# Cached attention pages with four neighbouring tokens to a partition, asked for and refilled in groups of four

## What is computed

```
k_past = cache_k[l, page_table].reshape(dec_b, past, 4, 128)      # past = 16 pages of 128 tokens
s = concat(q . k_past, q . k_new)                                 # per head and map
w = softmax(s * scale + bias)  of map 1  -  lam * the same of map 2
out = w[past] . v_past + w[new] . v_new
```

## Time and profile before

| what | us |
|---|---|
| median of 3 runs | 1985.19 |
| lowest and highest of them | 1980.44, 1985.21 |
| the profiled execution, its own time | 1986.06 |
| the profiled execution, its span from first to last instruction | 1984.5 |
| TensorE matmul busy | 1809.7 |
| weight loads of TensorE busy | 1656.1 |
| vector engine busy | 945.9 |
| scalar engine busy | 498.9 |
| key stretch, value stretch | 303 to 498, 498 to 612 |

### The profile page before, as it was taken

One profiled execution on the slowest core, in us unless ns is written; L12 is line 12 of the kernel. 1 busy time (PEld: TensorE's weight loads), 2 busy tenths in 40 slices (PEclk: granted clock), 3 DMA queues, 4 the chain that ended last, 5 costly groups with the idle time before them and its releaser, 6 DMA issues.

```text
span 1984.5 us, 32041 instructions
## 1 busy us (share of the span) xinstructions
PE 1809.7 (91%) x12995; PEld 1656.1 (83%) x12995; DVE 945.9 (48%) x1145; ACT 498.9 (25%) x861; POOL 117.3 (6%) x145
## 2 busy tenths in 40 slices
PE   6879998989988978898989879999999999999993
PEld 6779995656557968697779759999999999999982
DVE  5315888876765358422252393432323432333445
ACT  5111115666556221402431241110000010000122
POOL 2000001000220001001000020000000000000000
PEclk9889999999999989998999989999999999999995
DMA  5411216756785114213321121121111111111113
GB/s 177 134 44 59 69 64 204 204 166 199 247 300 188 64 46 145 107 43 127 128 86 43 42 88 43 43 63 43 42 43 42 44 63 43 43 42 37 48 44 131
DMA packets 137100, 187.80 MB, mean 95 GB/s; under 512 B 7720, under 2 KB 99050, under 8 KB 136486
## 3 DMA queue, kind: packets, MB, share of 16 engines
q1 hardware_dynamic: 122670, 121.47, 20.1%
q0 software_dynamic: 14192, 64.53, 9.2%
q10 hardware_dynamic: 144, 0.52, 0.1%
HBM read 166.17 MB, written 20.74 MB: 94 GB/s over the span
## 4 chain that ended last, share of the span: by engine, by line
PE 82%; DVE 7%; ACT 6%; issue 3%; DMA 2%; POOL 0%; SPq 0%; DVEq 0%; POOLq 0%; ACTq 0%
PE PS L1704 20%; PE PS L1705 19%; PE PS L1706 19%; PE PS L1694 7%; PE PS L1903 2%; PE PS L1925 2%; PE PS L1949 2%; DMA bias_rows<-BVEC 2%; PE PS L1824 2%; PE PS L2194 2%; ACT KTS L726 1%; PE PS L1986 1%; PE PS L1719 1%; PE PS L2215 1%; DVE Y L1225 1%
## 5 line engine op out<-in xcount | busy, mean ns | idle before, releaser
L1704 PE MATMUL PS<-XH,WH 128*128 128x352 f32 x1968 | 637.3, 324 | 18.8 <-ACT ST L726 18.8
L1705 PE MATMUL PS<-XL,WH 128*128 128x352 f32 x1968 | 632.4, 321 | 0.0
L1706 PE MATMUL PS<-XH,WL 128*128 128x352 f32 x1968 | 631.9, 321 | 0.0
L1125 DVE CAST WH<-RAW 128x1024 fp32r<-128x1024 f32 x126 | 94.2, 748 | 696.2 <-PE PS L1706 670.7
L1704 PEld LDWEIGHTS PS<-XH,WH 128*128 128x128 f32 x1968 | 370.4, 188 | 19.1 <-ACT ST L726 19.1
L1705 PEld LDWEIGHTS PS<-XL,WH 128*128 128x128 f32 x1968 | 371.1, 189 | 0.0
L1706 PEld LDWEIGHTS PS<-XH,WL 128*128 128x128 f32 x1968 | 370.2, 188 | 0.0
L1266 DVE SCALAR_TENSOR_TENSOR CY<-GP,DW,CY 128x1024 f32<-128x1024 f32 x124 | 158.5, 1278 | 1.0 <-DVE CY L1269 1.0
L1127 DVE TENSOR_TENSOR WL<-RAW,WH 128x1024 fp32r<-128x1024 f32 x126 | 156.5, 1242 | 4.3
L1704 PE MATMUL PS<-HH,WH 128*128 128x352 f32 x462 | 149.0, 323 | 0.0
L1705 PE MATMUL PS<-HL,WH 128*128 128x352 f32 x462 | 148.1, 321 | 0.0
(11 more groups left out here) (336 smaller groups left out, 2317.2 us busy)
## 6 DMA issues: line engine op xcount, KB each, us to landing
PG<-in_cache_k SPq DMA_DIRECT2D x128, 256.0 KB, 3.0
PG<-in_cache_v SPq DMA_DIRECT2D x64, 256.0 KB, 4.0
PG<-in_cache_v POOLq DMA_DIRECT2D x64, 256.0 KB, 4.2
RAW<-in_w_gate SPq DMA_DIRECT2D x22, 512.0 KB, 4.0
RAW<-in_w_up SPq DMA_DIRECT2D x22, 512.0 KB, 5.2
RAW<-in_w_in SPq DMA_DIRECT2D x20, 512.0 KB, 6.0
h_spill<-H POOLq DMA_DIRECT2D x2, 4224.0 KB, 11.9
H<-h_spill POOLq DMA_DIRECT2D x2, 4224.0 KB, 13.7
```

Source lines behind the costliest of these rows:

```text
L1125: dve.tensor_copy(WH[v % 2][:, :, :], raw).then_inc(hi_done, 1)
L1704: pe.matmul(out, WH[u][:, k, :], xh[:, k, cols], start=(k == 0), stop=False)
L1705: pe.matmul(out, WH[u][:, k, :], xl[:, k, cols], start=False, stop=False)
L1706: mm = pe.matmul(out, WL[u][:, k, :], xh[:, k, cols], start=False, stop=(k == kt - 1))
```

## The change

A page is read as 32 runs of four tokens, 8 KB each, to 32 partitions: page slot s goes to partitions 32 * (s mod 4) and the 31 behind it, into the four column blocks 4 * (s div 4) to the one 3 further. Four pages together fill the four column blocks on 128 partitions. What TensorE calls slot r is then column block r: every fourth token of each of the four pages of its group. Sums over tokens don't depend on the order, and keys and values have the same one. The near tokens are now on rows 96 to 127 of the last four column blocks, so EDGE is added there, in the same order of tokens.

Since a column block holds parts of four pages, TensorE waits for all four of a group, and a page may be overwritten only when all four column blocks of its group are used. There are 4 landing semaphores of each kind instead of 8, each for four slots. In the value stretch two of a group's pages come from SyncE and two from GpSimd, so every value page waits for both.

```diff
+        def page_rows(slot):
+            return PG[32 * (slot % 4):32 * (slot % 4) + 32, slot // 4 * 4:slot // 4 * 4 + 4, :]
+        def page_of(cache, page):
+            rows = cache[0].rearrange("n (i s) h d -> n i s (h d)", s=4)[ds(page, 1), :, :, :]
+            return rows.rearrange("n i s d -> (n i) s d")
...
-        pg_in = [sem(f"pg_in{i}") for i in range(PAGES // 2)]
-        vg_in = [sem(f"vg_in{i}") for i in range(PAGES // 2)]
+        pg_in = [sem(f"pg_in{i}") for i in range(PAGES // 4)]
+        vg_in = [sem(f"vg_in{i}") for i in range(PAGES // 4)]
...
-                src = cache[0].rearrange("n s h d -> n s (h d)")[ds(page, 1), :, :].rearrange("n s d -> (n s) d")
-                sp.dma_start(PG[:, slot, :], src).then_inc(pg_in[slot // 2], 16)
+                sp.dma_start(page_rows(slot), page_of(cache, page)).then_inc(pg_in[slot // 4], 16)
...
-                        sp.wait_ge(k_turned, PAGES * (n - 1) + r + 1)
+                        sp.wait_ge(k_turned, PAGES * (n - 1) + r // 4 * 4 + 4)
...
-                        sp.wait_ge(v_used, PAGES * (b - 1) + r + 1)
+                        sp.wait_ge(v_used, PAGES * (b - 1) + r // 4 * 4 + 4)
                     else:
-                        sp.wait_ge(k_turned, PAGES * (DB - 1) + r + 1)
+                        sp.wait_ge(k_turned, PAGES * (DB - 1) + r // 4 * 4 + 4)
...
-                        pool.wait_ge(v_used, PAGES * (b - 1) + r + 1)
+                        pool.wait_ge(v_used, PAGES * (b - 1) + r // 4 * 4 + 4)
...
-                    pool.dma_start(PG[:, r, :], src.rearrange("n s d -> (n s) d")).then_inc(vg_in[r // 2], 16)
+                    pool.dma_start(page_rows(r), page_of(io["cache_v"], page)).then_inc(vg_in[r // 4], 16)
...
-                dve.tensor_tensor(SD[:, g, (PAGES - 1) * P:PAGES * P], SD[:, g, (PAGES - 1) * P:PAGES * P], EDGE[:, :],
-                                  ALU.add).then_inc(sm_v, 1)
+                near = SD[:, g, (PAGES - 4) * P:PAGES * P].rearrange("p (s c) -> p s c", s=4)[:, :, 96:P]
+                dve.tensor_tensor(near, near, EDGE[:, :].rearrange("p (i s) -> p s i", s=4), ALU.add).then_inc(sm_v, 1)
...
-                pe.wait_ge(pg_in[r // 2], 32 * (n // PAGES) + 32)
+                pe.wait_ge(pg_in[r // 4], 64 * (n // PAGES) + 64)
...
-                if r % 2 == 0:
-                    pe.wait_ge(pg_in[r // 2], 32 * DB + 16 * (n // PAGES) + 16)
-                else:
-                    pe.wait_ge(vg_in[r // 2], 16 * (n // PAGES) + 16)
+                pe.wait_ge(pg_in[r // 4], 64 * DB + 32 * (n // PAGES) + 32)
+                pe.wait_ge(vg_in[r // 4], 32 * (n // PAGES) + 32)
```

More of the change, by code:

```diff
@@ L652, in _ @@
                     if b:
-                        pool.wait_ge(v_used, PAGES * (b - 1) + r + 1)
+                        pool.wait_ge(v_used, PAGES * (b - 1) + r // 4 * 4 + 4)
                     else:
-                        pool.wait_ge(k_turned, PAGES * (DB - 1) + r + 1)
+                        pool.wait_ge(k_turned, PAGES * (DB - 1) + r // 4 * 4 + 4)
                     page = pool.value_load(PT[:, PAGES * b + r:PAGES * b + r + 1], min_val=0, max_val=n_pages - 1)
-                    src = io["cache_v"][0].rearrange("n s h d -> n s (h d)")[ds(page, 1), :, :]
-                    pool.dma_start(PG[:, r, :], src.rearrange("n s d -> (n s) d")).then_inc(vg_in[r // 2], 16)
+                    pool.dma_start(page_rows(r), page_of(io["cache_v"], page)).then_inc(vg_in[r // 4], 16)
             pool.wait_ge(h_spilled, 16)
```

## The result

| | before | after |
|---|---|---|
| median of 4 runs, us | 1985.2 | 2015.67 |
| lowest and highest | 1980.44, 1986.15 | 2012.56, 2017.23 |
| profiled execution, us | 1986.06 | 2017.23 |
| its span | 1984.5 | 2015.4 |

The changed kernel takes 1.0156 times as long (95% interval 1.0135 to 1.0178), 30.5 us more. The prediction was 2008, with a range from 1987 to 2022. Medians and ratios of the experiments leave out three disturbed executions (one of e3, two of e8; 2327 to 3601 us).

What follows compares the result with a forecast made beforehand. TensorE was taken as nearly always busy, page transfers hidden beside it with little room in the value stretch. 21.3 + 2.5 - 1.2 = +22.6 us on 1986.06 gave 2008.7, so 2008 by the median; range 1987 to 2022.

Steps and rivals of the forecast that it cites:

- The mechanism that decides: Page transfers: landing on 32 partitions instead of 128, a page takes 1.16 us at about 226 GB/s.
- nearly all after 540: Sign of being right: transposes and products wait for pages, nearly all after 540 us.
- The value stretch: +21.3: Value stretch: 112 pages at 1.16 us after 501.9 end the last products at 632.9 instead of 611.65, +21.3 us.
- the first group's +2.5: Key stretch start: first transposes wait for four pages instead of two; +2.5 us, between 0 and 4.
- from there the transfers don't stop: Value stretch from 501.9 us: buffers wait for data, so pages follow without a gap at 1.16 us each.
- Refill by four: Key stretch: buffers are asked for up to three pages later, but 17 us of cover remain; nothing lost.
- -1.2: After the value stretch: the last slot's weights, waited for 1.23 us before, are no longer late; -1.2 us.
- The near-token add: Same 128x128 elements, 0.292 us, twice, with a split column pattern; cost 0, at most 0.6 us.
- Rival 1: Value stretch: both SBUF halves are written at once, faster than 270 GB/s; 1983 to 1999 us, chance 0.15.
- Rival 2: Value stretch: the halves overlap in part, 1.0 to 1.1 us a page; 1990 to 2001 us, chance 0.12.
- Rival 3: Page transfers are worse than the rows, 1.37 us a page, key stretch stalling too; 2032 us, chance 0.07.
- Rival 4: Page transfers: descriptors still move 2 KB, not 8 KB; the forecast holds, only packet counts would tell; no chance given.

Runs made afterwards that it cites:

- e3: Changed kernel with pages 1 and 2 of each group swapped, so the two queues write different halves of the SBUF in the value stretch; 2006.5 us.
- e8: From e1, key pages wait by two and refill singly, groups of four for value pages alone, all pages on 128 partitions; 1988.5 us.
- e6: Changed kernel with its 32-partition key pages, but value pages on 128 partitions, one token each; waits and refills by four stay; 1992.5 us.
- e4: Changed kernel with a page's 32 runs of 8 KB on every fourth partition of all 128; 1992.0 us.
- e12: Changed kernel with a page's 32 runs of 8 KB on every second partition of one half; 2016.5 us.
- e5: Changed kernel with a page as 64 runs of 4 KB on 64 neighbouring partitions of one half, buffers in groups of two; 1997.1 us.
- e11: e5 with another issue order: in the value stretch SyncE takes the first pair of each four pages, GpSimd the second; 1999.1 us.
- e9: Kernel before the change, with groups of four for key pages' waits and refills alone, all pages on 128 partitions; 1986.1 us.
- e1: Changed kernel's waits and refills by four, but pages on 128 partitions in 2 KB runs as before the change; 1990.9 us.
- e2: Changed kernel with four runs of 2 KB per partition instead of one of 8 KB, on the same 32 partitions; 2011.5 us.
- e13: e5 with a page's 64 rows on every second partition of all 128; 1984.0 us.
- e10: e3 with four runs of 2 KB per partition instead of one of 8 KB; 2004.2 us.

## Why the prediction was right, and where its sizes were off

**The mechanism that decides held.** Transfers to 32 partitions, priced from two small transfers that have nothing to do with pages, carry 222 GB/s at full share. The rows had given 228 to 233; the 226 was chosen a little under them, and that it came within 2% is partly luck. The key stretch stood it and the value stretch did not (e6); the first wait for a value page is at 544.05, as "nearly all after 540" had it. e4 and e12 show as the cause what two small transfers could only suggest, the place of the rows. The Trainium skill's 218 GB/s for 8 of 16 ports ("SBUF — State Buffer", "Door 1: The DMA port swizzle") agrees with 222 and 224 within 3%, and its map of ports with e4 and e12. Its sentence there that 64 partitions are no faster than 32 agrees with the landings in the key stretch (3.7 us in e5 against 3.8 in e12); the 255 and 250 GB/s of e5 and e11, with two queues, are above its 218, and no run here says why.

**The value stretch: +21.3 and the first group's +2.5 were taken up to its end; measured by the trace +28.8, and +30.0 if the earlier start of the stage is taken out.** The forecast had page 15 in at 501.9, which is 502.8 in the changed kernel's trace (2.0 later for the first group, 1.1 earlier for the stage), and no gap behind it. GpSimd's issues of page 15 and then of page 19, from two views of L665, show both:

```profile
L665 POOL DMA_DIRECT2D PG<-in_cache_v x1: 492/492/492, 497.8 to 497.8; - x1
...
DMA to landing us min/median/max: 6.0/6.0/6.0
...
L665 POOL DMA_DIRECT2D PG<-in_cache_v x1: 489/489/489, 503.5 to 503.5; - x1
...
DMA to landing us min/median/max: 6.3/6.3/6.3
```

Page 15 is in at 503.8, 1.0 late; it had been priced with the key pages' 3.0 us to landing, where value pages had 4.0. Page 19 is in at 509.8: four pages took 6.0 us instead of 4.6, so "from there the transfers don't stop" failed by 1.4 (from 500 to 510 us the share is 0.92). The rate takes 1.8 up to 544.05 (28 pages at 1.22 instead of 1.16) and 1.4 up to 638.23 (80 pages at 1.18). The last group's four pages end 640.49 - 638.23 = 2.3 us after the wait instead of 1.1, 1.2 more. Together that is 6.8, less 0.5 for the first group; 30.0 - 23.8 is 6.2.

**The first group: +2.5 was taken; the wait gives 2.0** in e9 (4.23 us instead of 1.88 and 0.36), and so does the first value product of the changed kernel. One execution doesn't fix it, though: from SyncE's first issue to the first value product e1 takes 1.5 and e9 4.5 us more than the kernel before. By time e9 costs 0.8 to 6.

**"Refill by four ... Nothing is lost there"** was worked out for the key stretch, and the sum has 0 for both. In the value stretch it is not 0. The step failed because no cover was worked out for that stretch; its mean rate, 0.88 us a page, would not have shown it, since it has a fast part: in the kernel before, 168 products (21 pages) start from 539.79 to 551.36 us, 0.6 us a page, and in e8 a group refilled by four comes 1.96 us late there. In the changed kernel the transfer waits begin before it, so it can't be seen there and did not spoil the forecast; with transfers on all partitions (e1, e4) it is the second part of what they lose.

**"-1.2" for the last slot's weights did not come, because they wait for the same pages.** TensorE still waits 0.79 us for them. The scalar engine in order of time:

```profile
639.32 0.37 ACT L733 ACTIVATE QK<-PS,SMALL 128x128 f32<-128x128 f32 x1 [3.40 <-PE PS L1932]
...
639.93 0.37 ACT L846 ACTIVATE PB<-PS,SMALL 128x128 f32<-128x128 f32 x1
```

Its copy ahead of the last exponentials waits 3.40 us for the products of L1932 at 638.57, which TensorE's order puts behind the page wait that ends at 638.23. So the weights move with the last pages and are not covered by them.

What follows the last value product is 2.1 us longer. A row says what goes with it: from 640 to 650 us the granted clock is 0.52, nearly all at the 1.2 GHz level, after the waits for pages. These waits do not always bring it. Busy time by stretch in e2, whose value stretch also ends in waits for pages:

```profile
640.00:650.00 10.00, 7.54 (x43) 5.79 (x43) 9.00 (x18) 8.44 (x13) 0.00 (x0) 1.00 0.04 12
```

The clock is full there, and what follows e2's last value product is 0.2 us longer than before. What decides between the two was not tried.

**The near-token add** takes 0.39 us instead of 0.29, by its line in the changed kernel and then in e2; nothing waits for it:

```profile
L1348 DVE TENSOR_TENSOR SD<-SD,EDGE x2: 390/394/398, 409.1 to 501.7; 128x128 f32<-128x128 f32 x2
...
L1348 DVE TENSOR_TENSOR SD<-SD,EDGE x2: 293/293/293, 410.5 to 503.1; 128x128 f32<-128x128 f32 x2
```

e2 has the same split columns of SD and reads EDGE in its own order, so the 0.1 us belong to reading EDGE at a step of four elements, not to the split.

Rival 1 would have needed 270 GB/s; even e3, its best case, gave 236. Rival 2's 1.0 to 1.1 us a page was not reached; e3 comes near it (262144 B at 236 GB/s, 1.11 us). Rival 3's 1.37 was not reached, and the key stretch is as long as it was. Rival 4 falls with the packets. So the forecast's time was 8 us low: 6.2 in the stretch and 3.3 after it (the 1.2 that did not come and 2.1 more), with the stage's earlier start (-1.1) against them.

## What to carry to other kernels

When a layout is changed for longer runs, look first at which partitions one transfer lands on: the same 8 KB runs cost 30 us on 32 neighbours and 7 on every fourth partition, of which the coarser groups by themselves cost 6. A transfer that is hidden by its stage's mean rate may not be in the stage's fastest ten microseconds; price buffers and refills there. A kernel's own small transfers, with share and rate read together, priced the large ones within 5% (228 to 233 against 222 GB/s).

## What the runs showed of the hardware

- A DMA share of 1.0 does not say how much is carried: 222 GB/s with 32 rows in one half (after), 396 in ten microseconds of e4 at 0.98. Read the two together.
- Where SyncE's queue alone loads pages, one with 64 rows in one half takes as long to land (3.7 us, e5) as one with 32 (3.8, e12), and one with 64 rows over all partitions less (3.2, e13).
- Two queues writing different halves do not add up to the whole rate: 236 (8 KB runs, e3), 244 (2 KB, e10), 255 GB/s (64 rows of 4 KB, e5). Why they stay so far under 396, and whether rows, runs or groups make 255 of 236, is open.
- The same bytes in 2 KB runs on the same 32 partitions went no slower than in 8 KB runs. By the rate of one execution each they went 2 to 3% faster (227 against 222, 244 against 236); the times don't tell them apart.
- A vector-engine add of 128x128 elements takes 0.39 us when it reads one input at a step of four elements (after), and 0.29 at a step of one (e2) or two (e5).
